# Gated unit's matmuls behind each step of the latent attention, and the experts' tokens kept in block order

## The reference, cut to what matters

```python
y = jax.nn.gelu(y_state_space + d_skip * xs)            # 256 tokens x 512
z = y @ w_glu + b_glu                                   # 512 -> 2048
val, gate = jnp.split(z, 2, axis=-1)
y_ssm = val * jax.nn.sigmoid(gate)                      # the gated unit
q_lat = einsum('blhd,chd->blhc', q, w_uk) * 64 ** -0.5  # 8 heads
p = softmax(q_lat . c_kv, over the 64 chosen keys)      # the latent attention
y_att = einsum(p . c_kv, w_uv) @ w_attn_proj
merged = sigmoid(ga) * y_ssm + sigmoid(gb) * y_att
h = h + gate1 * (merged @ w_out)                        # then the feed-forward part
```

## Time and profile before

| | us |
|---|---|
| median of three runs (lowest, highest) | 2119.44 (2118.46, 2121.9) |
| the profiled execution: time, span | 2120.8, 2119.0 |
| PE busy | 1858.1 (88% of the span) |
| DVE, ACT, POOL busy | 897.5, 653.0, 550.6 |
| mean rate of the transfers | 271 GB/s over the span |

### The profile page before, as it was taken

How to read it: one execution, slowest core, us unless ns; L and a number is a source line. 1 busy time by engine, 2 the same in 40 slices (tenths; PEclk the granted TensorE clock), 3 DMA queues, 4 the chain that set the end, 5 groups by cost and what they waited for, 6 DMA issues and landing times.

```text
span 2119.0 us, 56357 instructions
## 1 busy us (share of the span) xinstructions
PE 1858.1 (88%) x23140; PEld 1327.0 (63%) x23141; DVE 897.5 (42%) x2115; ACT 653.0 (31%) x1228; POOL 550.6 (26%) x407
## 2 busy tenths in 40 slices
PE   5999979999999997998989976767659997899998
PEld 3444457666676675745776754545536775678886
DVE  2098154555555555446244422222246954210001
ACT  1001144445445444215244422222242222120001
POOL 0000014666666662001024422222265001000000
PEclk8999979999999999999999989888869998899999
DMA  9664163989999999822189999999982166233320
GB/s 375 227 239 159 40 270 147 382 340 421 421 419 423 418 423 399 317 80 70 41 329 421 403 419 423 422 424 421 422 313 95 65 238 239 100 135 121 123 98 20
DMA packets 133060, 574.35 MB, mean 271 GB/s; under 512 B 4720, under 2 KB 9840, under 8 KB 116464
## 3 DMA queue, kind: packets, MB, share of 16 engines
q1 hardware_dynamic: 132688, 570.72, 68.1%
q10 hardware_dynamic: 288, 2.43, 0.3%
HBM read 572.08 MB, written 1.05 MB: 270 GB/s over the span
## 4 chain that ended last, share of the span: by engine, by line
PE 66%; DMA 18%; DVE 7%; ACT 3%; SPq 3%; issue 3%; DVEq 0%; ACTq 0%
PE bank L339 25%; PE bank L545 17%; DMA ring<-in_expert_w_down 16%; PE bank L496 6%; PE bank L517 5%; PE bank L908 3%; SPq L2122 3%; DVE b L948 2%; ACT b L1669 2%; PE bank L593 2%; PE bank L410 1%; PE bank L826 1%; DMA ring<-in_conv_w_in 1%; DMA ring<-in_attn_w_in 1%; DVE b L1485 1%
## 5 line engine op out<-in xcount | busy, mean ns | idle before, releaser
L545 PE MATMUL bank<-ring,b 128*32 128x128 f32 (+1 forms) x13600 | 528.6, 309 | 117.3 <-issue 48.0
L545 PEld LDWEIGHTS bank<-ring,b 128*32 128x32 f32 x13600 | 401.6, 115 | 300.1 <-issue 209.6
L948 DVE TENSOR_TENSOR h_t<-h_t,bank 128x512 f32<-128x512 f32 (+1 forms) x696 | 350.7, 566 | 509.2 <-PE bank L517 509.2
L1669 ACT ACTIVATE b<-bank 128x128 f32<-128x128 f32 (+3 forms) x546 | 185.7, 366 | 1092.5 <-PE bank L496 410.5
L339 PE MATMUL bank<-h_t,ring 128*128 128x256 f32 (+1 forms) x1728 | 472.1, 436 | 8.3 <-DVE h_t L1452 3.6
L339 PEld LDWEIGHTS bank<-h_t,ring 128*128 128x128 f32 x1728 | 335.5, 195 | 137.8 <-issue 96.6
L2070 POOL TENSOR_SCALAR b<-b 128x1024 f32<-128x1024 f32 (+1 forms) x85 | 195.1, 2295 | 72.2 <-POOL b L2078 37.1
L2078 POOL TENSOR_TENSOR b<-b 128x512 f32<-128x512 f32 (+1 forms) x85 | 89.6, 1054 | 428.3 <-PE bank L517 428.3
L1669 ACT ACTIVATE b<-b 128x256 f32 (+5 forms) x186 | 181.7, 1020 | 29.6 <-DVE b L948 16.3
L517 PE MATMUL bank<-b 32*128 32x512 f32 (+1 forms) x1392 | 172.6, 567 | 5.5 <-DVE h_t L948 4.8
L2073 POOL TENSOR_TENSOR b<-b,b 128x1024 f32<-128x1024 f32 (+1 forms) x85 | 161.3, 1898 | 7.1
(11 more groups left out here) (270 smaller groups left out, 1475.8 us busy)
## 6 DMA issues: line engine op xcount, KB each, us to landing
ring<-in_expert_w_gate SPq DMA_DIRECT2D x64, 2048.0 KB, 13.4
ring<-in_expert_w_up SPq DMA_DIRECT2D x64, 2048.0 KB, 15.7
ring<-in_expert_w_down SPq DMA_DIRECT2D x64, 2048.0 KB, 15.8
ring<-in_ada_w SPq DMA_DIRECT2D x24, 2048.0 KB, 19.5
ring<-in_w_mod SPq DMA_DIRECT2D x12, 2048.0 KB, 7.8
ring<-in_w_in SPq DMA_DIRECT2D x6, 2048.0 KB, 12.3
ring<-in_conv_w_in SPq DMA_DIRECT2D x5, 2048.0 KB, 8.8
ring<-in_w_ffn_gate SPq DMA_DIRECT2D x5, 2048.0 KB, 7.7
```

Of the source, the lines that this page charges most:

```text
L545: last = pe.matmul(b[32 * m:32 * m + 32, 0:width], lhs[:, k, :], rhs[:, k, m * width:(m + 1) * width], start=(k == 0), stop=(k == nk - 1), ...
L948: return dv.tensor_tensor(o, a, b, op)
L1669: return ac.activation(o, i, f, **kw)
```

## The change

The gated unit's 16 groups no longer stand ahead of the latent attention: group u follows `latent_weigh(u)` in step u. Four of the six pieces go ahead of the loop, the other two follow steps 5 and 11. The weight chunks of the ring are listed in the new order. DVE divides first in each step (`normalise2(u)`, then `take_query` and `soften2(u + 1)`). ACT copies the values and the probabilities first, then does the next exponential, then empties the group of the gated unit, always with Identity; the Sigmoid of all of `sig` (128x2048) is one operation after the loop, and POOL waits for it (`gate_open`). `atto` moves to another buffer, since `sig` stays where `atto` was. Two semaphores of the router become one that counts to 2.

In the experts, `h_tok` is kept block by block (block k holds the features 8p + k). ACT's copies out of PSUM now write with a step of 128 elements (512 bytes), and the first dispatch and `take_h` read side by side.

```diff
-    after += cols(w["w_ssm_glu_2"][0], [0, 1024, 2048]) + pieces[30:] + cols(w["w_attn_proj_2"][0], [0, 1024])
+    after += pieces[30:34] + cols(w["w_ssm_glu_2"][0], [0, 1024, 2048]) + pieces[34:] + cols(w["w_attn_proj_2"][0], [0, 1024])
...
-        atto = v3(h_t, 2048, 4, SEQ)
+        atto = v3(b3, 0, 4, SEQ)
...
-                    dispatch(bank[q], lambda t, kk: h_tok[:, t, 2 * q + kk:D:KD], 0)
+                    dispatch(bank[q], lambda t, kk: h_tok[:, t, (2 * q + kk) * P:(2 * q + kk + 1) * P], 0)
...
-            glu(0)
-            glu(1)
...
+            for p in LATENT[:4]:
+                piece_step(p)
             latent_query(0)
             latent_score(0)
             for u in range(16):
...
                 latent_weigh(u)
-                if u % 2 and u < 13:
-                    piece_step(LATENT[u // 2])
+                glu(u // KD, u % KD)
+                if u in (5, 11):
+                    piece_step(LATENT[4 + u // 6])
...
             for u in range(16):
+                normalise2(u)
                 if u % 2 == 0 and u < 14:
                     take_query(u // 2 + 1)
                 if u < 15:
                     soften2(u + 1)
-                normalise2(u)
...
-                    b, t, cols = full(), i // 2, slice(i % 2 * 512, (i % 2 + 1) * 512)
-                    taken(act(h_tok[:, t, cols], b[:, :], ACT.Copy))
+                    b, t, half = full(), i // 2, i % 2
+                    rows = h_tok[:, t, :].rearrange("p (k q) -> p q k", k=KD)
+                    taken(act(rows[:, 64 * half:64 * half + 64, :], b.rearrange("p (q k) -> p q k", k=KD), ACT.Copy))
...
-                    src = h_tok[:, 0:tiles, :].rearrange("p t (d k) -> p t k d", k=KD)[:, :, bass.ds(q * 2, 2), :]
-                    act(v4(h_q, 0, 4, 2, P)[:, 0:tiles], src, ACT.Copy) \
+                    act(v3(h_q, 0, 4, 256)[:, 0:tiles], h_tok[:, 0:tiles, bass.ds(q * 256, 256)], ACT.Copy) \
...
+            for p in LATENT[:4]:
+                piece_step(p)
             exponential(0)
             for u in range(16):
-                if u < 15:
-                    exponential(u + 1)
-                if u == 3:
-                    ac.wait_ge(sem("gated_ssm"), 1)
                 if u >= 3 and u % 2:
                     take_values((u - 3) // 2)
                 b, t = full(), u % 2
                 taken(act(p2_t[t].rearrange("p k n -> p (k n)")[:, 0:reach[t]], b[:, 0:reach[t]], ACT.Copy))
-                if u % 2 and u < 13:
-                    piece_step(LATENT[u // 2])
+                if u < 15:
+                    exponential(u + 1)
+                b, m = full(), u % KD
+                taken(act((val, sig)[u // KD][:, m, :], b[:, 0:SEQ], ACT.Identity, bias=pr("b_glu", u, 1)))
+                if u in (5, 11):
+                    piece_step(LATENT[4 + u // 6])
             take_values(7)
+            ac.wait_ge(a_free, marks["glu1"][1])
+            act(sig, sig, ACT.Sigmoid).then_inc(sem("gate_open"), 1)
             take_turned(LATENT[-1])
...
-            po.wait_ge(a_free, marks["glu1"][1])
+            po.wait_ge(sem("gate_open"), 1)
```

More of the change, by code:

```diff
@@ L209, in piece_chunk @@
                 return start["middle"] + p - 18
-            return start["middle"] + 13 + p - 24 if p < 30 else start["after"] + 13 + p - 30
+            return start["middle"] + 13 + p - 24 if p < 30 else start["after"] + 11 + p - 30 + 2 * (p >= 34)
         cond_pad, cond2_pad = v3(sm, 72, KD, 32), v3(par, PARAM_AT["c_im"][0], KD, 32)
@@ L469, in moe @@
                 if layer == 0:
-                    pe.wait_ge(sem("later_ready"), 1)
+                    pe.wait_ge(sem("order_ready"), 1)
                     group("v", lambda b: pe.matmul(b[:, 0:NE + 1], n_chunks[0:NE, NE:NE + 1].broadcast_to([NE, P]),
                                                    later[0:NE, :], start=True, stop=True))
-                    pe.wait_ge(sem("base_ready"), 1)
+                    pe.wait_ge(sem("order_ready"), 2)
                     def bases(b):
@@ L816, in _, with glu, emit @@
             channel_out(in_projection_last, "a", lambda k: U[:, k, :], KD, 512, SEQ)
-            def glu(j):
-                loaded(n + 7 + j)
-                wt = chunk(n + 7 + j, 4, 1024)
-                for m in range(KD):
-                    def emit(b):
-                        for k in range(4):
-                            if m == 0:
-                                pe.wait_ge(sem("y_gelu"), k + 1)
-                            last = pe.matmul(b[:, 0:SEQ], wt[:, k, m * P:(m + 1) * P], y_ssm[:, k, :],
-                                             start=(k == 0), stop=(k == 3))
-                        return last
-                    group("a", emit)
-                done_with(n + 7 + j)
+            def glu(j, m):
+                if m == 0:
+                    loaded(n + 11 + j)
+                wt = chunk(n + 11 + j, 4, 1024)
+                def emit(b):
+                    for k in range(4):
+                        if j == 0 and m == 0:
+                            pe.wait_ge(sem("y_gelu"), k + 1)
+                        last = pe.matmul(b[:, 0:SEQ], wt[:, k, m * P:(m + 1) * P], y_ssm[:, k, :],
+                                         start=(k == 0), stop=(k == 3))
+                    return last
+                group("a", emit)
+                if m == KD - 1:
+                    done_with(n + 11 + j)
                 mark(f"glu{j}")
-            glu(0)
-            glu(1)
             def latent_query(h):
@@ L1073, in moe @@
                     do(dv.tensor_scalar(place, place, place_end, 0.0, ALU.min, ALU.max))
-                    dv.tensor_scalar(later, cn("iota", 0, NE + 1), place, None, ALU.is_gt).then_inc(sem("later_ready"), 1)
+                    dv.tensor_scalar(later, cn("iota", 0, NE + 1), place, None, ALU.is_gt).then_inc(sem("order_ready"), 1)
                     step(dv.tensor_copy(se, v3(b, 0, tiles, NE)))
@@ L1986, in _ @@
             gate_projection(sgb, 4, KD)
-            for m in range(KD):
-                b = full()
-                taken(act(val[:, m, :], b[:, 0:SEQ], ACT.Identity, bias=pr("b_glu", m, 1)))
-            for m in range(KD):
-                b = full()
-                taken(act(sig[:, m, :], b[:, 0:SEQ], ACT.Sigmoid, bias=pr("b_glu", 8 + m, 1)))
             def exponential(u):
```

2 lines of the change are left out of this document (1 added, 1 removed).

## The result

The changed kernel takes 2092.66 us (median of four, 2090.18 to 2093.62), against 2118.95 (four, 2114.63 to 2121.9) for the kernel before beside it: a ratio of 0.9878, with an interval of 0.9864 to 0.9892. The profiled execution took 2092.63 us, its span is 2090.8, so between the two profiled executions 28.2 us went.

A forecast was written before the change was run, and what follows sets the result against it. The chain of waits was taken to go through TensorE for two thirds, transfers for 18%. Second block 14.4 us less, dispatches 5.5 and 2.0 less, copies 6.6 more: 15.3 less, 2104.1 us, range 2094 to 2112.

The forecast's parts named there:

- (c): Latent attention's loop: TensorE's own work sets the pace, 62.0 us together, plus 2.0 for one fall to half clock.
- (g): Experts' first dispatch, read side by side: 5.5 us less in layer 0 and 2.0 less in layer 1.
- (i): Experts' routing: ACT's copies writing with a step cost 0.55 us more each, 6.6 us more in both layers.
- (a): Ahead of the loop: four pieces and three transposes, 8.3 us, hidden by DVE's mask.
- (b): Start of the latent chain: 3.9 us from the query's copy to the first weigh, some 13 us after the input projection's end.
- Do the waits go?: Latent loop: TensorE's 3.7 us a step exceeds the part of DVE's and ACT's 3.2 it needs, helped by the new order.
- (d): End of the stage: last mix to `latent_out` 1.6 us, then ACT's values, table load, Sigmoid and last copy 4.1.
- (e): POOL's two products, now starting with the Sigmoid's end, finish 7 us before the projection ends: no cost.
- (f): Transfers: pieces needed 28 us or more earlier still arrive, and SP's longer wait for gated chunks' slots costs nothing.
- writes with a step are free: Rival on ACT's copies in the experts: no added cost, 21.9 us less in all, 2097.5; chance 0.33.
- the dear writes: Rival on ACT's copies: strided writes much dearer than reads, 4.2 ns more an element making the kernel 0.2% slower; chance 0.04.
- the waits stay: Rival on the latent loop: TensorE still waits in every step, 11.7 us come back, 2115.8; chance 0.10.

The follow-up runs named there:

- e4: The changed kernel with all six pieces inside the loop, each behind an odd step, and none ahead of it: 2102.27 us.
- f2: The changed kernel with eight matmuls in each gated group, its four done twice: 2117.75 us, the loop 81.75 us against 54.43.
- e3: The changed kernel with DVE's old order in the loop (query's copy, next softening, then the division): 2108.51 us.
- e6: The changed kernel with the reordering copy's loops swapped, so ACT reads PSUM with the step and writes side by side: 2087.62 us.
- e1: The changed kernel with the experts' tokens in the old order, so only the second block is changed: 2098.53 us.
- e5: The changed kernel with ACT's copy of the last turned piece moved ahead of the Sigmoid and its table load: 2089.01 us.
- e2: The kernel before with only the experts' part of the change: 2112.25 us.

## Why the prediction was wrong

The direction and the places were right, and the gain came out 11 us too small. Two terms of the sum failed in their size: TensorE's own work in the loop, (c), which was put too high, and the experts' part, (g) and (i), which was put at 0.9 us and gave 5.9. By the medians the block gave 19.6 where 14.4 were forecast, and the experts 5.9 where 0.9 were: 5.2 and 5.0 too little, nearly the whole miss. By the two traces the block's share is larger, 10.0. By the forecast's own steps:

(a) Pieces hidden: 8.9 us instead of 8.3, with a pause of 0.37 in them. The pause stands behind the same record of the fourth piece in all other traces with the pieces ahead, with 0.56 to 0.94 us; its cause is open. DVE's mask hides the pieces but for 0.3 us (its query's copy waits 0.34), and e4 shows what they cost without it.

(b) First weigh 12.7 us behind the input projection's end; 13.0 forecast.

(c) is the step that failed most, in its size: "3.9 us for two steps, 31.2 for 16", "one fall to half clock" and "I take 2.0". Together its sum has 64.0 us from the first weigh to the last gated group, and the loop took 54.4. The 3.9 was read from steps in which TensorE waited, as the time less the waits that the view of PE listed. The true work of two steps is 3.10, as the changed kernel's rows show and f2 confirms. The difference of 0.8 is short waits, and rows that follow each other less closely. The largest part is 0.31 at the mix. Before, it starts 0.53 us behind the score, and ACT's rows and those of the weight loads show why:

```profile
1797.21 0.39 PE L846 MATMUL bank<-b,b 128*128 128x128 f32 x2
1797.41 0.28 ACT L1669 ACTIVATE b<-bank 128x128 f32<-128x128 f32 x1 [0.18 <-PE bank L410]
1797.74 0.30 PEld L339 LDWEIGHTS bank<-b,b 128*128 128x128 f32 x2 [0.33 <-ACT b L1669]
1797.74 0.49 PE L339 MATMUL bank<-b,b 128*128 128x128 f32 x2
```

The mix waits for ACT's copy of the probabilities just turned, and PE's own row lists no wait, only that of the weight load does. In the changed kernel this copy lies under the gated group, and the mix starts 0.22 us behind the score (1736.67 to 1736.89). The other mix is 0.16 longer before (0.61 from 1795.26 to 1797.05, less the wait of 1.18, against 0.45), and the remaining rows together 0.3.

Eight times 0.8 is 6.4 us. Another 1.8 were counted wrongly. Two queries and two scores stand ahead of the first weigh, 2.0 us and not 1.2, and the last mix and `latent_out` (1.0) are in (c) and again in (d). Against it the gated groups took 28.2 us by their starts, not 27.7. That makes 7.6 to 7.7. The 2.0 for the clock did not come at all: the first wait of the loop was 0.75 us long, and the window shows 1.00 from the start. In sum (c) was 9.6 us too high, which is nearly all of the 10.0 by which the stage gained more between the traces. That the medians show only 5.2 of it lies with the stage before, not with the new one, whose length agrees within 0.6 us in three traces (72.7, 73.3 and 73.1). What in the stage before makes up the rest stays open.

"Do the waits go?" They went, but the reason given was half of it. TensorE does set the pace; but had DVE's order stayed, the waits would have too (e3), although a step then held 3.3 us of TensorE's work, more than the chain's 2.3. Of the forecast's sentence on "the new order" this was the weightier part, and it got no price.

(d) The end: 5.6 us, 5.7 forecast, with 0.3 instead of 0.5 for the last copy and the start behind it.

(e), (f) and (h) cost nothing, as forecast. The projection did not wait for POOL, no wait of TensorE in the stage is put down to a transfer (only the cause of the pause in (a) is open), and layer 0's loop of experts took 489.0 us before and 489.9 in the changed kernel, so the shorter `take_h` gained nothing.

(g) First dispatch: 5.4 less between the two executions, 5.9 by the means; 5.5 forecast. In layer 1 the way to the first gate was 4.1 us shorter, where 2.0 were forecast: the half clock was thought to stay, and the granted clock was 1.00 in this dispatch (1092.6 to 1096.5).

(i) Copies: 3.2 and 1.7 us longer, 4.4 and 2.2 forecast. On the way from the copies (layer 0) or the first piece (layer 1) to the dispatch it was 1.9 and 2.6 us by the means, the latter with more half clock in it. So (g) and (i) together are 4.6 us better than their sum: 10.0 gained instead of 7.5, and 4.5 lost instead of 6.6. The experts give 5.9 by the medians, not 0.9; the last 0.4 of the difference lie in no place that the traces show.

The rival "writes with a step are free" would have given 2097.5 and stands nearer to the result, by luck: its mechanism is refuted, as the write costs 0.40 us a copy. That of the dear writes is refuted too (0.78 ns more an element, not 4.2 and more). The rival that the waits stay did not come either; e3 shows that with DVE's old order it would have.

## What to carry to other kernels

Don't take an engine's own work from a stretch in which it waits, by subtracting the waits that are listed: short waits stay in it. Take it from a dense stretch of the same instructions, or sum up the pitch of rows that follow each other at once, look at the rows of the weight loads for waits too, and count each piece of work once.

Where an engine waits for a chain, ask at which instruction the chain begins. If that is one which the waiting engine issues itself just ahead of the wait, work that is put behind the wait doesn't shorten it, and changing the other engine's order does (1.0 us a step here, with the gated groups to fill the steps, and 0.55 without them).

A reordering copy has its step on one side or the other, by the order of its two loops. Try both (here 5.0 us). And an engine's small last copy, for which others wait, belongs ahead of its long operation.

## What the runs showed of the hardware

ACT's copy out of PSUM of 128x512 costs 0.40 us more with a step of 512 bytes in the write to SBUF (7.23 against 4.03 us for eight), which is 0.78 ns an element, and nothing more with a step of 32 bytes in the read of PSUM (4.03). The same step of 32 bytes in ACT's read of SBUF had 1.07 ns, and 48 such copies fell from 2142 to 1043 ns each when the change made them read side by side. The Trainium skill's page "PSUM — Partial Sum Buffer", section "Specifications (TRN2)", gives PSUM lines of 8 bytes and says that non-contiguous access slows matmuls a lot; for ACT's read of PSUM, e6 shows no such cost.

TensorE's weights of 128x128 float32, read with a step of 32 bytes, take the same time at either clock. Layer 1's dispatch had 7.88 us before, with 10 records in 1.90 us at a granted clock of 0.50, and 7.85 us in e1, where the clock was 1.00 throughout:

```profile
1092.49 7.85 PE L496 MATMUL bank<-b,b 128*128 128x128 f32 x32 [0.31 <-DVE b L1133]
```

That is 245 ns a record. Side by side the same 32 records take 3.81 us in the changed kernel, 119 ns each, at a clock of 1.00.

DVE's addition of 128x24 took 4.40 us beside POOL's product in the changed kernel, and 0.18 us in e5, where POOL started later. It began 0.15 us behind the product and ended with it. The Trainium skill's page "SBUF — State Buffer", section "SBUF: two separate sides", calls the pair of ports that the two engines share an exclusive lock, which one holds for the whole instruction while the other is blocked; the two rows agree.

A kernel's profiled executions differ by up to 5.6 us ahead of the stage with the same code (1710.7 to 1716.3). About half of it can arise in one place, where TensorE's clock falls in the routing: from layer 1's first piece to its first dispatch it took 26.8 to 27.2 us in five executions and 29.5 to 29.7 in three. In the changed kernel, one of the three, the granted clock was 0.50 from 1083 to 1087; in e2, one of the five, it was 0.96 from 1077 to 1081, at the same matmuls. An effect of 5 us spread over such a place needs means over several executions.
